# Two directions of a linear attention: own buffers for each, and its preparation placed between the retention's head norms and the masks

## What is computed

```python
def gla_scan(q, k, v, log_a, s0):          # 4 heads, key width 64, value width 128, CHUNK = 64
    def step(s, inp):
        qc, kc, vc, ac = inp
        G = jnp.cumsum(ac, axis=2)
        G_last = G[:, :, -1:, :]
        q_t = qc * jnp.exp(G)
        k_t = kc * jnp.exp(-G)
        scores = jnp.where(causal, jnp.einsum("bhid,bhjd->bhij", q_t, k_t), 0.0)
        out = (jnp.einsum("bhij,bhjv->bhiv", scores, vc)
               + jnp.einsum("bhid,bhdv->bhiv", q_t, s))
        s = (jnp.exp(G_last[:, :, 0, :])[..., None] * s
             + jnp.einsum("bhjd,bhjv->bhdv", kc * jnp.exp(G_last - G), vc))
        return s, out
...
    ret = head_rmsnorm(o_rf + flip_seq(o_rb)) * jax.nn.silu(rg)
    gla = head_rmsnorm(o_gf + flip_seq(o_gb)) * jax.nn.silu(gg)
```

## Time and profile before

| | us |
|---|---|
| median of 3 runs | 3232.37 |
| lowest and highest | 3221.74, 3232.96 |
| the profiled execution, its own time | 3232.67 |
| span of the profiled execution, first to last instruction | 3230.7 |
| TensorE matmul, busy | 2772.9 (86%) |
| VectorE, busy | 1693.5 (52%) |
| ScalarE, busy | 890.3 (28%) |
| GpSimd, busy | 1148.9 (36%) |
| DMA, mean over the span | 224 GB/s |

### The profile page before, as it was taken

How to read it: one execution, slowest core, us unless ns; L and a number is a source line. 1 busy time by engine, 2 the same in 40 slices (tenths; PEclk the granted TensorE clock), 3 DMA queues, 4 the chain that set the end, 5 groups by cost and what they waited for, 6 DMA issues and landing times.

```text
span 3230.7 us, 30180 instructions
## 1 busy us (share of the span) xinstructions
PE 2772.9 (86%) x11160; PEld 1895.2 (59%) x11160; DVE 1693.5 (52%) x3622; ACT 890.3 (28%) x1683; POOL 1148.9 (36%) x763
## 2 busy tenths in 40 slices
PE   6999999979979999889985879998877777777876
PEld 3999989967557887678834655544323223222322
DVE  3666651022737611121045267776777777777765
ACT  3111131124532223222131233323222222222221
POOL 1222223224823444322110145544544444444441
PEclk8999999989999999989986889999999999999999
DMA  5555522212015422212100249999999999999996
GB/s 200 162 178 176 182 99 60 61 59 72 14 65 164 163 104 83 80 53 66 41 34 1 66 165 380 392 410 427 427 427 427 427 427 427 427 427 427 427 427 289
DMA packets 126957, 722.12 MB, mean 224 GB/s; under 512 B 15204, under 2 KB 17516, under 8 KB 60140
## 3 DMA queue, kind: packets, MB, share of 16 engines
q0 software_dynamic: 73728, 536.90, 39.8%
q1 hardware_dynamic: 37448, 127.67, 11.6%
q10 hardware_dynamic: 15652, 55.90, 5.5%
HBM read 718.31 MB, written 2.10 MB: 223 GB/s over the span
## 4 chain that ended last, share of the span: by engine, by line
PE 58%; DMA 27%; DVE 9%; ACT 3%; issue 2%; POOL 0%; SPq 0%; DVEq 0%; ACTq 0%; POOLq 0%
PE acc L568 14%; PE acc L570 13%; PE acc L569 13%; DMA arena<-in_peer_rows,squares 8%; DMA wring<-in_peer_rows,squares 7%; DMA hid<-in_peer_rows,squares 6%; PE sums L1022 5%; PE acc L1022 2%; DMA resid<-in_peer_rows,squares 2%; PE sums L509 2%; DMA modw<-in_peer_rows,squares 2%; DVE hid L1663 2%; DVE hid_parts L1669 1%; ACT hid L1084 1%; PE acc L757 1%
## 5 line engine op out<-in xcount | busy, mean ns | idle before, releaser
L2386 POOL TENSOR_TENSOR wring_parts<-wring,wring_parts 128x1024 fp32r<-128x1024 f32 (+1 forms) x215 | 517.1, 2417 | 1335.3 <-ACT wring_parts L1084 1335.2
L568 PE MATMUL acc<-hid_parts,wring_parts 128*128 128x384 f32 (+2 forms) x2088 | 780.4, 374 | 81.4 <-DVE hid_parts L1669 60.9
L570 PE MATMUL acc<-hid_parts,wring_parts 128*128 128x384 f32 (+2 forms) x2088 | 756.8, 362 | 0.0
L569 PE MATMUL acc<-hid_parts,wring_parts 128*128 128x384 f32 (+1 forms) x1656 | 601.3, 363 | 0.0
L568 PEld LDWEIGHTS acc<-hid_parts,wring_parts 128*128 128x128 f32 (+1 forms) x2088 | 397.7, 190 | 157.7 <-issue 70.3
L570 PEld LDWEIGHTS acc<-hid_parts,wring_parts 128*128 128x128 f32 (+1 forms) x2088 | 398.2, 191 | 37.1
L1084 ACT ACTIVATE wring_parts<-wring 128x1024 fp32r<-128x1024 f32 (+1 forms) x215 | 222.1, 1040 | 595.7 <-DMA wring<-in_w_ffn_out 219.3
L569 PEld LDWEIGHTS acc<-hid_parts,wring_parts 128*128 128x128 f32 x1656 | 316.5, 191 | 31.8 <-issue 5.5
L2398 POOL DMA_INDIRECT arena<-in_peer_rows,squares x180 | 199.9, 1110 | 238.1 <-PE acc L1022 144.5
L1084 ACT ACTIVATE hid<-hid 128x2 f32<-128x2 f32 (+2 forms) x292 | 65.5, 224 | 761.1 <-DVE arena L2221 243.7
L2398 POOL DMA_INDIRECT wring<-in_peer_rows,squares x158 | 173.6, 1099 | 204.8 <-PE acc L1022 150.7
(11 more groups left out here) (382 smaller groups left out, 4412.2 us busy)
## 6 DMA issues: line engine op xcount, KB each, us to landing
wring<-in_w_ffn_in SPq DMA_DIRECT2D x88, 512.0 KB, 5.4
modw<-in_w_ada ACTq DMA_DIRECT2D x56, 512.0 KB, 3.8
modw<-in_w_mod ACTq DMA_DIRECT2D x48, 512.0 KB, 3.9
wring<-in_w_ffn_out SPq DMA_DIRECT2D x32, 512.0 KB, 3.5
wring<-in_w_in SPq DMA_DIRECT2D x28, 512.0 KB, 3.4
wring<-in_w_mix_in SPq DMA_DIRECT2D x18, 512.0 KB, 3.4
wring<-in_peer_w_q SPq DMA_DIRECT2D x16, 512.0 KB, 5.8
hid<-in_w_ada SPq DMA_DIRECT2D x6, 1024.0 KB, 17.3
```

The source lines that it names most:

```text
L568: nc.tensor.matmul(o, wh, high, start=first, stop=False)
L569: nc.tensor.matmul(o, wh, low, start=False, stop=False)
L570: return nc.tensor.matmul(o, wl, high, start=False, stop=last)
L2386: nc.gpsimd.tensor_tensor(Wlor[:, p, 0:blocks, 0:cols], Wlo[:, p, 0:blocks, 0:cols], Whir[:, p, 0:blocks, 0:cols], ALU.subtract).then_inc( ...
```

## The change

Each direction gets its own `gG`, `gE`, `gkt`, `gS`, `gla_decay`, `gkd`, `gqz` and `gP`, in memory that is free at the time (among it `squares`, `modw` and the retention's `rq`); `gkd_tok` stays shared. The code of VectorE and ScalarE is cut into small functions, and their calls stand in a new order. The wait of the queries of d = 1 for four outputs is gone. ScalarE squares one head ahead (`later=1`). TensorE's list keeps its order. No operation is added or left out. The diff, without the definitions that only repeat the old lines under a name:

```diff
-        gG, gE, gkt, gS = ar(6144, 2, TC), ar(7680, 2, TC), ar(9216, 2, T), ar(10240, 2, NCH, P)
-        gla_decay = dec[:, 48:64].rearrange("p (a c) -> p a c", a=2)
-        gkd, gkd_tok, gqz, gP = hi(0, 2, TC), hi(1536, 6, 256), hi(3072, 4, T), hi(5120, 2, T)
+        gG, gE = [ar(6144, 2, TC), hi(6144, 2, TC)], [ar(7680, 2, TC), hi(10240, 2, TC)]
+        gkt, gS = [ar(9216, 2, T), hi(9216, 2, T)], [ar(10240, 2, NCH, P), ar(6144, 2, NCH, P)]
+        gla_decay = [dec[:, 48 + 16 * d:64 + 16 * d].rearrange("p (a c) -> p a c", a=2) for d in range(2)]
+        gkd = [hi(0, 2, TC), squares[:, 0:2 * TC].rearrange("p (a t) -> p a t", a=2)]
+        gkd_tok, gqz = hi(1536, 6, 256), [hi(3072, 4, T), ar(4096, 4, T)]
+        gP = [hi(5120, 2, T), modw[:, 0:2 * T].rearrange("p (a t) -> p a t", a=2)]
...
-            def inverse(t, used, of=None):
-
-                act.wait_ge(sq_used, n.sq)
+            def inverse(t, used, of=None, later=0):
+
+                act.wait_ge(sq_used, n.sq - later)
...
-            for h in range(4):
-                def head(j, h=h):
-                    act.wait_ge(o_copied, 9 + h)
-                    return rq[:, h, :]
-                stat(1, T, head, 13 + h)
...
+            def head_squared(h):
+                act.wait_ge(o_copied, 9 + h)
+                squared(rq[:, h, :], T)
...
-                if d:
-                    act.wait_ge(acc_ready, UNIT["gla0"] + 2)
...
+            head_squared(0)
+            head_squared(1)
+            inverse(T, 13, later=1)
+            gla_gates(0)
+            head_squared(2)
+            inverse(T, 14, later=1)
+            gla_inverse_gates(0)
+            head_squared(3)
+            inverse(T, 15, later=1)
+            gla_state_gates(0)
+            inverse(T, 16)
+            gla_tokens(0)
+            gla_gates(1)
+            gla_inverse_gates(1)
+            gla_state_gates(1)
+            gla_tokens(1)
...
+            def ret_norm(h):
                 head_norm(rq[:, h, :], yT[:, h, :])
...
+            def to_chunk_end(d):
+                for pr in range(2):
+                    G4 = chunks(gG[d][:, pr, 0:T])
+                    ins = V.tensor_tensor(chunks(gE[d][:, pr, 0:T]), G4[:, :, CHUNK - 1:CHUNK].to_broadcast([P, NCH, CHUNK]), G4, ALU.subtract)
+                    if d == 0:
+                        ins = V.tensor_tensor(gE[d][:, pr, T:TC], gG[d][:, pr, TC - 1:TC].to_broadcast([P, C]), gG[d][:, pr, T:TC], ALU.subtract)
+                if d == 0:
+                    ins.then_inc(gla_arg, 1)
+                else:
                     link(ins)
-                    for pr in range(2):
-                        ins = V.tensor_tensor(gE[:, pr, 0:T], gE[:, pr, 0:T], la[:, d, pr, 0:T], ALU.add)
-                    ins.then_inc(gla_arg, 1)
-                    dve.wait_ge(gla_o, 4)
-                e = gE if d == 0 else gkd
+
+            def with_own_token():
+                for pr in range(2):
+                    ins = V.tensor_tensor(gE[1][:, pr, 0:T], gE[1][:, pr, 0:T], la[:, 1, pr, 0:T], ALU.add)
+                ins.then_inc(gla_arg, 1)
+
+            def without_own_token():
+                dve.wait_ge(gla_qk, 12)
+                for pr in range(2):
+                    ins = V.tensor_tensor(gE[1][:, pr, :], gG[1][:, pr, :], la[:, 1, pr, :], ALU.subtract)
+                ins.then_inc(gla_arg, 1)
+
+            def gated_queries(d):
+                e = gE[0] if d == 0 else gkd[1]
                 dve.wait_ge(gla_exp, 3 * d + 1)
                 for h in range(4):
-                    V.scalar_tensor_tensor(gqz[:, h, :], gq[:, h // 2, :], c_("head_rows")[:, h % 2:h % 2 + 1], e[:, h // 2, 0:T],
+                    V.scalar_tensor_tensor(gqz[d][:, h, :], gq[:, h // 2, :], c_("head_rows")[:, h % 2:h % 2 + 1], e[:, h // 2, 0:T],
                                            ALU.mult, ALU.mult).then_inc(gla_qk, 1)
+
...
+            def causal(d, h):
                 mask = c_(("causal_f", "causal_b")[d]).bitcast(I32).unsqueeze(1).to_broadcast([P, 4, P])
-                for h in range(4):
-                    u = base + 5 + h
-                    b = unit(u)
-                    if h >= 2:
-                        dve.wait_ge(gla_o, 4 * d + h - 1)
-                    free(V.copy_predicated(gP[:, h % 2, :].rearrange("p (r n) -> p r n", r=4), mask,
-                                           acc[:, b, :].rearrange("p (r n) -> p r n", r=4)), u)
+                u = UNIT[f"gla{d}"] + 5 + h
+                b = unit(u)
+                if h >= 2:
+                    dve.wait_ge(gla_o, 4 * d + h - 1)
+                free(V.copy_predicated(gP[d][:, h % 2, :].rearrange("p (r n) -> p r n", r=4), mask,
+                                       acc[:, b, :].rearrange("p (r n) -> p r n", r=4)), u)
+
+            dve.wait_ge(o_ready, 8 + 24)
+            gla_sums(0)
+            ret_norm(0)
+            gated_queries(0)
+            ret_norm(1)
+            gated_keys(0)
+            dve.wait_ge(gla_qk, 6)
+            to_chunk_end(0)
+            ret_norm(2)
+            state_keys(0)
+            ret_norm(3)
+            gla_sums(1)
+            states(0)
+            causal(0, 0)
+            to_chunk_end(1)
+            causal(0, 1)
+            with_own_token()
+            causal(0, 2)
+            gated_queries(1)
+            causal(0, 3)
+            gated_keys(1)
+            without_own_token()
+            state_keys(1)
+            states(1)
+            for h in range(4):
+                causal(1, h)
```

More of the change, by code:

```diff
@@ L1476, in _, with gla_gates, gla_inverse_gates, gla_state_gates @@
             ret_out(3)
-            for h in range(4):
-                def head(j, h=h):
-                    act.wait_ge(o_copied, 9 + h)
-                    return rq[:, h, :]
-                stat(1, T, head, 13 + h)
-            for d in range(2):
-                base = UNIT[f"gla{d}"]
-                e = (gE if d == 0 else gkd)[:, :, 0:T]
-                g = (gG if d == 0 else gE)[:, :, 0:T]
+            def head_squared(h):
+                act.wait_ge(o_copied, 9 + h)
+                squared(rq[:, h, :], T)
+            def gla_gates(d):
                 act.wait_ge(gla_arg, 2 * d + 1)
-                run(gla_decay,
-                    gG[:, :, 0:T].rearrange("p a (c i) -> p a c i", i=CHUNK)[:, :, :, CHUNK - 1],
+                run(gla_decay[d],
+                    gG[d][:, :, 0:T].rearrange("p a (c i) -> p a c i", i=CHUNK)[:, :, :, CHUNK - 1],
                     ACT.Exp, scale=1.0 / GATE_NORM)
-                if d:
-                    act.wait_ge(acc_ready, UNIT["gla0"] + 2)
-                run(e, g, ACT.Exp, scale=1.0 / GATE_NORM).then_inc(gla_exp, 1)
+                e, g = (gE[0], gG[0]) if d == 0 else (gkd[1], gE[1])
+                run(e[:, :, 0:T], g[:, :, 0:T], ACT.Exp, scale=1.0 / GATE_NORM).then_inc(gla_exp, 1)
+            def gla_inverse_gates(d):
                 act.wait_ge(gla_qk, 6 * d + 4)
-                run(e, g, ACT.Exp, scale=-1.0 / GATE_NORM).then_inc(gla_exp, 1)
+                e, g = (gE[0], gG[0]) if d == 0 else (gkd[1], gE[1])
+                run(e[:, :, 0:T], g[:, :, 0:T], ACT.Exp, scale=-1.0 / GATE_NORM).then_inc(gla_exp, 1)
+            def gla_state_gates(d):
                 act.wait_ge(gla_arg, 2 * d + 2)
-                run(gE, gE, ACT.Exp, scale=1.0 / GATE_NORM).then_inc(gla_exp, 1)
+                run(gE[d], gE[d], ACT.Exp, scale=1.0 / GATE_NORM).then_inc(gla_exp, 1)
+            def gla_tokens(d):
                 for pr in range(2):
-                    u = base + pr
+                    u = UNIT[f"gla{d}"] + pr
                     b = unit(u)
@@ L2018, in chunks, with gla_sums @@
                 return x1.rearrange("p (c i) -> p c i", i=CHUNK)
-            dve.wait_ge(o_ready, 8 + 24)
-            for d in range(2):
-                base = UNIT[f"gla{d}"]
+            def gla_sums(d):
                 for pr in range(2):
-                    ins = V.tensor_tensor_scan(gG[:, pr, :], c_("chunk_reset"), la[:, d, pr, :], 0.0, ALU.mult, ALU.add)
+                    ins = V.tensor_tensor_scan(gG[d][:, pr, :], c_("chunk_reset"), la[:, d, pr, :], 0.0, ALU.mult, ALU.add)
                 if d == 0:
@@ L2029, in _ @@
                     link(ins)
-                    for pr in range(2):
-                        G4 = chunks(gG[:, pr, 0:T])
-                        ins = V.tensor_tensor(chunks(gE[:, pr, 0:T]), G4[:, :, CHUNK - 1:CHUNK].to_broadcast([P, NCH, CHUNK]), G4, ALU.subtract)
-                    link(ins)
-                    for pr in range(2):
-                        ins = V.tensor_tensor(gE[:, pr, 0:T], gE[:, pr, 0:T], la[:, d, pr, 0:T], ALU.add)
-                    ins.then_inc(gla_arg, 1)
-                    dve.wait_ge(gla_o, 4)
@@ L2059, in _, with states @@
+            def states(d):
+                base = UNIT[f"gla{d}"]
                 u = base + 2
```

35 lines of the change are left out of this document (14 added, 21 removed).

## The result

The changed kernel takes 3194.13 us (median of 9 runs, 3186.36 to 3215.71) against 3229.76 us for the kernel before (9 runs, 3220.68 to 3239.57). The ratio is 0.9907, with a 95% interval from 0.9888 to 0.9925: 24 to 36 us faster. Measured twice more, on the same code, it was 0.9942 (0.9924 to 0.9959) and 0.9924 (0.9900 to 0.9949). The mean of the three ratios says some 24 us; the medians of the first set, 35.6 us apart, say more than the other two bear out (19.7 and 22.1).

The account below looks back on a forecast made before the run. The prediction took a stretch of engine hand-overs, with nothing saturated, to delay everything behind it. 3232.67 - 16.7 (part 1) - 10.9 (part 2) - 0.7 (clock) = 3204.4 us, range 3193 to 3214.

Parts of the forecast that it names:

- Where the bound is: Stretch from 1690 to 1786 us: a chain of hand-overs with nothing saturated; shortening it moves all that follows equally forward.
- Part 1: From last retention output to first direction's state keys: head norms interleaved with its preparation, keys start 16.7 us earlier.
- The cover ahead of the states: VectorE's extra work between first state keys and state additions fits within TensorE's 9.0 us, with 0.8 us left.
- Squaring ahead, priced at nothing: Retention head norms: the old pitch of 4.04 us already delivers the inverses; issuing the second square ahead only makes that earlier.
- they end last nowhere but at the first: The four head norms' inverses hold VectorE up only at the first norm, at 1690.0 us.
- Part 2: From first direction's masks to second's state keys: second direction prepared beside the first's outputs, 10.9 us less.
- Clock, -0.7 us: TensorE in the stretch: shorter pause keeps the second transposes warm; half of their 1.4 us gain taken, 0.7 us less.
- The worst end: TensorE's clock in the stretch: three warm groups of some 1.1 us turn cold, +3 us.
- Only part 1: Rival, 0.06: VectorE's insertions delay masks and TensorE's outputs one for one, second direction's change gives nothing; 3216 us.
- Nothing follows: Rival, 0.03: something behind the stretch, a gather or weight load, sets the end anyway; 3232 us.
- Clock lost through to w_out: Rival, 0.02: TensorE stays at 1.2 GHz through both directions and into w_out; 3233 us, up to 3273.
- Clock high throughout: Rival, 0.12: shorter pauses keep TensorE's clock high throughout the stretch, 6.3 us below the forecast; 3198 us.

Follow-up runs that it names:

- eleven memsets: The changed kernel with eleven more 0.91 us memsets on VectorE just ahead of the first state keys: 3212.95 us, ratio 0.9961 to the kernel before.
- part2_only: The changed kernel with the first direction's preparation back in the old order, four head norms first; own buffers kept: 3218.64 us, ratio 0.9971 to the kernel before.

## Why the prediction was right, point by point

- **Where the bound is.** Right. A stretch that is a relay gave its time to the whole kernel one for one, as the eleven memsets show from the other side: their 12.8 us lie in the first window, and the part behind the stretch kept its length.
- **Part 1, 16.7 us.** Measured 16.6. State keys 13.9 us after the copy, as laid out, in every execution of this order.
- **The cover ahead of the states, 0.8 us.** Right for the clock of before's execution only. In the changed kernel's first two profiles the additions waited 0.95 and 0.96 us for TensorE (in the first, the copy of the first state ended at 1713.21 and they started at 1714.16). In the third, TensorE's products for the context's state ran at 2.4 GHz (1.12 us instead of 2.00), the additions started right behind VectorE's copy, 22.1 us after the last retention copy instead of 23.0, and TensorE itself had stood for that copy:

```profile
1698.58 1.10 PE L936 MATMUL acc<-arena,hid 64*64 64x128 f32 x32 [1.00 <-DVE arena L2095]
```

  So the cover of 0.8 us is gone where TensorE is fast, and more than 0.9 us of a faster clock does not get through ahead of the first additions.
- **Squaring ahead, priced at nothing.** Wrong, without harm to the sum. The step that failed took the old pitch of 4.04 us from a list in which nothing stood between the norms. It asked only when VectorE wants an inverse; that TensorE's transposes stand behind the fourth mean, and so wait for its inverse, was not seen. Squaring ahead is worth 4.0 us, and even with it that inverse releases the transposes in every profile of the changed kernel. So "they end last nowhere but at the first" does not hold, though it costs only 0.04 us there (1.26 us from state keys to transposes, 1.22 before).
- **Part 2, 10.9 us.** Right in mechanism. The second state keys were forecast 43.7 us after the copy; they came at 46.6, 43.8 and 43.4 us. The pause before the second transposes was forecast at 1.4 us and measured 1.15, 1.34 and 1.35. The waits of the transposes (L914, now L917) add up to 3.3 to 3.7 us, 4 forecast. By the state keys part 2 gave 8.1, 10.9 and 11.3 us. The third mask of the first profile waits 4.86 us for scores, never for VectorE, as required.
- **Clock, -0.7 us.** This term was mis-sized, and on the mean of three of the wrong sign. Against the 72.3 us of the sum without a clock term, the three stretches are +3.9, +1.2 and -1.4 us. The worst end was put at +3, by three groups of some 1.1 us; it is output 0 of the first direction and the scores behind it that turn cold, 1.90 and 1.11 us in before's execution, 3.51 and 2.02 in the changed kernel's first. Of the 0.7 us that the transposes were to gain, 0.2 to 0.4 came: they took 2.58, 2.62 and 2.41 us instead of 2.82. The Trainium skill (TensorE: Matmul & The Clock Gate, "HAM oscillation") warns of long idle gaps and wants the array kept at work. The traces agree in that work in the pauses keeps the clock up: 1.00 in the first window with filling products, 0.62 to 0.64 without. That shorter pauses keep it up by themselves is not what the runs show: TensorE's longest pause in the changed kernel's stretch was 2.3 us, instead of 17.4, and its clock in the windows was 0.62 to 0.87, against 0.56 to 0.82 before.
- **The whole, 3204.4 us, 28.3 us less.** The measurements are 30, 19 and 24 us less, the stretches 23.7, 26.4 and 29.0. The first median, 3194.13, lies 10 us below the forecast and 1 us above the lower bound of the range, and that it lies inside is luck: the bound was 3193 because one run before had come in low, and what makes such runs was not forecast. The stretches explain at most 29.0 of its 35.6 us. The repeats' medians, 3208.57 and 3206.50, lie 2 to 4 us above the forecast.
- **The rivals.** Only part 1: refuted by part2_only and by the two windows. Nothing follows: refuted. Clock lost through to w_out: refuted, from the second output of a direction on the products took 1.90 us in every profile. Clock high throughout: no profile of the changed kernel shows it, and with work put there for it the windows came to 1.00, 0.94 and 0.93.

## What to carry to other kernels

A stretch in which the engines mostly wait for each other is a relay. Its new length could here be summed to a tenth of a microsecond from the durations of the old trace where VectorE bounds it (16.7 us forecast, 16.6 measured), and not where TensorE's clock does: lay out the two chains side by side, let each wait of one hold work of the other, and ask of every list, the third engine's too, what now stands behind what. Own buffers gave nothing by themselves, but in part 2 they are what lets the order change (whether part 1 needs them was not tried); the gain then comes from the order, and one square issued a step ahead was worth a quarter of the larger move. Where short bursts of TensorE alternate with pauses, do not trust one profile to a few microseconds: profile the same code three times before a difference of that size is given a cause.

## What the runs showed of the hardware

- The first window of the changed order took 15.19 us in four profiles (the three of the changed kernel, and the one with filling products), to the hundredth, though TensorE's clock was 0.62 in one and 1.00 in another. In the stretch VectorE's and ScalarE's durations were the same from execution to execution within some hundredths; TensorE's nearly doubled. That is not so everywhere: early in the kernel two VectorE products on a weight tile took 2.86 and 2.82 us in one profile and 0.74 in the next.
- 16 output products of 128x64 took 3.51 us at a granted clock of 0.50 (1.2 GHz) and 1.90 at 1.00 (2.4 GHz). Which of them are slow differs between executions of identical code (3.51, 1.90 and 2.14 us for output 0 in three profiles).
- A memset of 0.91 us that VectorE must see finished before its next one has a pitch of 1.19 us.
- With no pause of TensorE above 2.3 us, the granted clock over the changed kernel's windows was 0.62 to 0.87; with 128x128 products of no use in the pauses it was 1.00, 0.94 and 0.93.
